# Four Silu tiles, a root and seven modulation sums moved to other places of a two-layer kernel

## The reference

```python
mod = jax.nn.silu(c) @ w_ada[l] + b_ada[l]
sh1, sc1, g1, sh2, sc2, g2 = jnp.split(mod[:, None, :], N_MOD, axis=-1)
u = rmsnorm(h, norm1_w[l]) * (1.0 + sc1) + sh1
proj = u @ w_in[l]
hq, hf, hi, hg, aq, ak, av = jnp.split(proj, offs, axis=-1)
o_hg = hgrn2(hq, hf, hi, hg, lower_bounds[l], hgrn_gnorm_w[l])   # ends: rmsnorm(o, w) * silu(hg)
o_da = diff_attention(aq, ak, av, lam, lambda_init, diff_subln_w[l])
mix = jnp.concatenate([o_hg, o_da.astype(o_hg.dtype)], axis=-1) @ w_out[l]
h = h + g1 * mix
u = rmsnorm(h, norm2_w[l]) * (1.0 + sc2) + sh2
ff = (jax.nn.silu(u @ w_ffn_gate[l]) * (u @ w_ffn_up[l])) @ w_ffn_down[l]
h = h + g2 * ff
```

## Time and profile before

| | us |
|---|---|
| median of three runs | 1548.53 |
| the profiled execution, device time | 1550.16 |
| its span | 1548.4 |
| TensorE arrays busy | 1470.0 (95%) |
| DVE busy | 984.9 (64%) |
| ACT busy | 448.9 (29%) |
| modulation sums, 80 on line 1622 (the first 16 have a line of their own) | 103.2 |

### The profile page before, as it was taken

The page is one execution under the profiler, slowest core; times in us unless marked ns, Lnnn a source line. Parts: engine busy times, 40 slices in busy tenths (PEclk is TensorE's granted clock), DMA queues, the critical chain, the costliest instruction groups (busy, mean ns, idle before and its releaser), DMA issues.

```text
span 1548.4 us, 19571 instructions
## 1 busy us (share of the span) xinstructions
PE 1470.0 (95%) x7186; PEld 1176.7 (76%) x7186; DVE 984.9 (64%) x1727; ACT 448.9 (29%) x921; POOL 95.6 (6%) x75
## 2 busy tenths in 40 slices
PE   3989999898999999998999999999998999999997
PEld 2777866576888888887876666778886888888886
DVE  8789878777676666556546666875555444444342
ACT  5333354423222221002234445531113222222011
POOL 0100000020000000221700000000030000000110
PEclk9999999998999999998999999999998999999999
DMA  9243233333655555443221111113322223233322
GB/s 368 82 155 109 68 107 111 109 110 122 203 180 201 189 192 181 143 137 122 70 82 42 42 42 42 55 49 102 109 95 68 96 94 106 84 108 88 99 88 92
DMA packets 52611, 175.80 MB, mean 114 GB/s; under 512 B 5953, under 2 KB 6337, under 8 KB 52545
## 3 DMA queue, kind: packets, MB, share of 16 engines
q1 hardware_dynamic: 52544, 174.94, 34.6%
HBM read 172.82 MB, written 2.10 MB: 113 GB/s over the span
## 4 chain that ended last, share of the span: by engine, by line
PE 51%; ACT 1%; DVE 1%; issue 0%; ACTq 0%; DVEq 0%
PE bank L623 11%; PE bank L625 11%; PE bank L624 11%; PE bank L1065 8%; PE bank L1084 2%; PE bank L1119 2%; PE bank L1096 2%; PE bank L635 1%; PE bank L636 1%; PE bank L637 1%; PE bank L996 0%; DVE wl L1602 0%; PE bank L1109 0%; PE bank L1040 0%; PE bank L732 0%
## 5 line engine op out<-in xcount | busy, mean ns | idle before, releaser
L623 PE MATMUL bank<-uh,wh 128*128 128x512 f32 x808 | 316.4, 392 | 6.0 <-DVE wl L1602 4.8
L625 PE MATMUL bank<-uh,wl 128*128 128x512 f32 x808 | 315.4, 390 | 0.0
L624 PE MATMUL bank<-ul,wh 128*128 128x512 f32 x808 | 315.3, 390 | 0.0
L1600 DVE CAST wh<-wraw 128x1024 fp32r<-128x1024 f32 (+1 forms) x235 | 156.0, 664 | 198.4 <-PE bank L625 179.7
L1602 DVE TENSOR_TENSOR wl<-wraw,wh 128x1024 fp32r<-128x1024 f32 (+1 forms) x235 | 274.0, 1166 | 8.1
L623 PEld LDWEIGHTS bank<-uh,wh 128*128 128x128 f32 x808 | 152.1, 188 | 39.0 <-issue 4.9
L624 PEld LDWEIGHTS bank<-ul,wh 128*128 128x128 f32 x808 | 152.2, 188 | 31.5
L625 PEld LDWEIGHTS bank<-uh,wl 128*128 128x128 f32 x808 | 152.1, 188 | 31.5
L623 PE MATMUL bank<-hh,wh 128*128 128x512 f32 x352 | 137.7, 391 | 0.0
L625 PE MATMUL bank<-hh,wl 128*128 128x512 f32 x352 | 137.2, 390 | 0.0
L624 PE MATMUL bank<-hl,wh 128*128 128x512 f32 x352 | 137.1, 390 | 0.0
(11 more groups left out here) (353 smaller groups left out, 2385.2 us busy)
## 6 DMA issues: line engine op xcount, KB each, us to landing
ada<-in_w_ada_dram SPq DMA_DIRECT2D x96, 512.0 KB, 4.6
wraw<-in_w_in_dram SPq DMA_DIRECT2D x61, 512.0 KB, 3.4
wraw<-in_w_ffn_gate_dram SPq DMA_DIRECT2D x44, 512.0 KB, 3.3
wraw<-in_w_ffn_up_dram SPq DMA_DIRECT2D x44, 512.0 KB, 3.3
wraw<-in_w_ffn_down_dram SPq DMA_DIRECT2D x32, 512.0 KB, 3.5
wraw<-in_w_ffn_down_dram SPq DMA_DIRECT2D x16, 384.0 KB, 3.1
wraw<-in_w_out_dram SPq DMA_DIRECT2D x16, 256.0 KB, 2.8
wraw<-in_w_out_dram SPq DMA_DIRECT2D x8, 512.0 KB, 3.3
```

The lines of the kernel that those rows point to most:

```text
L623: nc.tensor.matmul(bank[:], a, rh[:, k0 + k, :], start=(first and k == 0), stop=False)
L624: nc.tensor.matmul(bank[:], a, rl[:, k0 + k, :], start=False, stop=False)
L625: mm = nc.tensor.matmul(bank[:], b, rh[:, k0 + k, :], start=False, stop=(last and k == nk - 1))
L1600: V.tensor_copy(wh[:, slot, 0:n], wraw[:, slot, 0:n]).then_inc(w_hi, 1)
```

## The change

- The Silu of the four gate tiles, with its table load and a load of the exponential's table behind it, moves on ACT from behind the last drain of `a1` to the last head of the recurrence, ahead of exponential 7.
- The Silu of `scb[:, 1]` (the second block's `c`) moves from there to the place ahead of `ff1`.
- The square root of the head sums and its table loads move on ACT from ahead of step 0 to the end of step 1. On DVE the guard moves from step 0 to step 1, the root's reciprocal from step 1 to step 2, and the scaling of the heads from steps 2 to 5 to steps 3 to 6.
- Modulations 24 and 25 move ahead of the two last splits in the last head, 26 and 27 behind the last merge of the last head. The steps 0, 2, 4, 6 and 8 have one modulation each instead of two (28 to 32), steps 10, 12, 14 and 16 have 33 to 36 (before: two in 10, 12 and 14), and 37 to 39 go behind the splits of units 1 to 3 of `out1`. The second norm's gain moves from ahead of `out1` to its unit 5.

```diff
+        MOD_AHEAD = {PH["a1"].u0 + 13: [24], PH["da1"].u0: [25]}
+        MOD_STATES = {PH["da1"].u0 + 1: [26, 27]}
         for n_ in range(5):
-            MOD_AFTER[PH["da1"].u0 + n_ + 1] = [24 + 2 * n_, 25 + 2 * n_]
+            MOD_AFTER[PH["da1"].u0 + n_ + 1] = [28 + n_]
+        for n_ in range(4):
+            MOD_AFTER[PH["out1a"].u0 + n_] = [33 + n_]
         for n_ in range(3):
-            MOD_AFTER[PH["out1a"].u0 + n_] = [34 + 2 * n_, 35 + 2 * n_]
+            MOD_AFTER[PH["out1"].u0 + n_ + 1] = [37 + n_]
...
-                for j in MOD_AFTER.get(u - 2, ()):
+                for j in itertools.chain(MOD_AHEAD.get(u - 2, ()), MOD_STATES.get(u - 2, ()), MOD_AFTER.get(u - 2, ())):
...
                 for lv in range(1, 8):
+                    if h == HEADS1 - 1 and lv == 7:
+                        for n in range(HEADS1):
+                            A(p1[:, 12 + n, :], p1[:, 12 + n, :], ACT.Silu).then_inc(silu_ok, 1)
+                        nc.scalar.preload_act_table_set("natural_log_exp_and_others")
                     exp_level(h, lv)
...
                     a1_drain(A1_UNITS - 1)
-                    for n in range(HEADS1):
-                        A(p1[:, 12 + n, :], p1[:, 12 + n, :], ACT.Silu).then_inc(silu_ok, 1)
-                    act.wait_ge(c_land[1], 16)
-                    A(scb[:, 1, :], scb[:, 1, :], ACT.Silu).then_inc(c_silu, 1)
...
-            nc.scalar.preload_act_table(ACT.Sqrt)
-            act.wait_ge(rs_ok, 2)
-            A(rsh[:, 0:16], ssh[:, 0:16], ACT.Sqrt, bias=epst, scale=SQ_BACK / P).then_inc(rs_ok, 1)
...
                     A(p1[:, TILES["da1"][n], :], B[1][:], ACT.Copy).then_inc(drain_a, 1)
+                if m == 1:
+                    nc.scalar.preload_act_table(ACT.Sqrt)
+                    act.wait_ge(rs_ok, 2)
+                    A(rsh[:, 0:16], ssh[:, 0:16], ACT.Sqrt, bias=epst, scale=SQ_BACK / P).then_inc(rs_ok, 1)
+                    nc.scalar.preload_act_table_set("natural_log_exp_and_others")
...
             norm_u(1, mod1[:, 24:32])
+            act.wait_ge(c_land[1], 16)
+            A(scb[:, 1, :], scb[:, 1, :], ACT.Silu).then_inc(c_silu, 1)
             ffn("ff1", 0)
...
                 u = PH["a1"].u0 + n + 1
+                for j in MOD_AHEAD.get(u, ()):
+                    modulation(j)
                 split(u, u % 2)
...
                     exponents(0)
+                else:
+                    for j in (26, 27):
+                        modulation(j)
...
-                if m == 0:
+                if m == 1:
                     guard_sums(hg, 0)
...
-                if m == 1:
+                if m == 2:
                     root_sums(hg, 0)
-                if 2 <= m <= 5:
-                    head_normed(m - 2)
+                if 3 <= m <= 6:
+                    head_normed(m - 3)
...
-            v.wait_ge(mod_done, 40)
-            gains(1, mod1, vt1, NORM_B, 32)
...
                 add_out1(PH["out1"], t, OUT1_BANKS[t])
+                if t == 5:
+                    v.wait_ge(mod_done, 40)
+                    gains(1, mod1, vt1, NORM_B, 32)
```

More of the change, by code:

```diff
@@ L8 @@
+import itertools
 from contextlib import ExitStack
```

## The result

Five runs of each kernel on one chip: 1539.98 us median (1538.91 to 1542.15) after, 1548.53 (1547.54 to 1550.27) before; the ratio is 0.9946, 95% interval 0.9934 to 0.9957. Five more runs of the changed kernel gave 1540.86 and a ratio of 0.9941 (0.9927 to 0.9954). The forecast was 1538.3 in a range of 1534.5 to 1543.5, so the median came 1.7 us later than said. The profiled execution took 1538.91, with a span of 1537.2 against 1548.4.

The account below looks back on a forecast made before the run. TensorE ends the program but stalls in attention steps, on ACT at step 2 and DVE at 8, 12 and 16. Profiled 1550.16 less 10.2 gave 1540.0; on the median, 1538.3, range 1534.5 to 1543.5.

Parts of the forecast that it names:

- biased scores 7: DVE's biased scores for attention step 7, forecast to start at 245.4 instead of 251.90.
- wait at step 8: TensorE's wait ahead of step 8's output, forecast at 1.9 us instead of 2.88, with the clock falling again.
- waits at step 12: TensorE's two waits at step 12, forecast at 0.3 instead of 1.50 and 1.4 for the drain, clock staying up.
- The sum to step 16: Total gain over the attention steps up to TensorE's start at 299.37 in step 16: minus 10.2 us.
- DVE's term for step 14: Step 14's modulation is on the path; one fewer gains 1.2 us more, leaving 2.9 of wait at step 16.
- Rival 1: Only the opening is gained, fewer modulations buy nothing behind step 3: 5.9 to 6.5 us, so 1542.3; chance 0.16.
- Rival 2: The clock stays up at step 8, where half clock costs 1.8 us: gain 12.0, so 1536.5; chance 0.15.
- The terms for steps 2 and 12: Half clock expected to vanish from TensorE's stretches behind the waits of steps 2 and 12: 2.8 and 1.2 us.
- 1.2 us of cover: Idle time left on ACT behind the 4.8 us Silu block, ahead of the last head's exponential 7; block costs nothing.
- The price put on a broken cover: If ACT's idle time in the last head did not cover the Silu block, it would cost up to 4.8 us.
- Cost 0; 3.6 at most: Three modulations behind the output projection's splits fit DVE's idle time: cost 0, at most 3.6 us.
- a late unit of the output projection: Sign of being wrong: an output projection unit coming late; one late through the load queue would cost 1 to 2 us.

Follow-up runs that it names:

- collide: The kernel before with modulation 39 moved from step 14 beside GpSimd's add in the output projection, second norm's gain behind unit 5; one run, 1548.03 us.
- mods_only: The kernel before with only the modulations moved to their new places and the second norm's gain at unit 5; 1541.10 us, ratio 0.9946.
- mods_late: The changed kernel with the modulations of steps 6, 10 and 14 moved behind the splits of steps 8, 12 and 16; 1535.75 us, ratio 0.9912.
- drain_first: The changed kernel with ACT's drain of bank 1 ahead of the four squares in steps 7 and 11; 1536.13 us, ratio 0.9913.
- act_only: The changed kernel with modulations back in their old places, keeping ACT's edits, the guard's move and the norm gain at unit 5; 1546.05 us, ratio 0.9975.
- head_load: The changed kernel with two more ACT table loads behind the four Silus of the last head; 1543.89 us, ratio 0.9963; repeated, ratio 0.9964.
- out1_early: The changed kernel with two of three modulations taken out of the output projection's second half, 39 behind unit 1's split; 1538.16 us, ratio 0.9925.

## Why the forecast was right, and where it was off

In the frame of the profile before (0.72 later than the profile after):

| step | forecast | measured |
|---|---|---|
| biased scores 1 | 214.6 | 214.6 |
| drain of bank 1 starts | 217.2 | 217.3 |
| scores 3 | 221.4 | 221.5 |
| waits at steps 3 and 4 | 0.2, 0.75 | 0.20, 0.75 |
| biased scores 7 | 245.4 | 245.5 |
| wait at step 8, and from its end to the filling | 1.9, 2.1, clock falls | 1.84, 2.17, falls |
| waits at step 12 | 0.3, 1.4, clock stays | 0.29, 1.41, stays |
| wait at step 16, its end | 2.9, 289.2 | 2.88, 288.6 |

(The prediction's own terms for biased scores 7 add up to 245.5.)

**The attention steps.** Each step of the chain held, with the reasons given: who is late at which step was read from what ended the idle time, and what comes next from the rows of later steps with the same shapes. The sum to step 16 was 10.2; counted from the first scores it is 10.8, of which 0.4 is a fall of the clock at step 8 that was shorter than before's (4.70 against 5.07). DVE's term for step 14 stands alone in collide: with one modulation gone from there, the wait at step 16 is 2.87 instead of 4.07. Rival 1 is excluded by mods_only and mods_late; what it says of ACT's squares ahead of the drain holds for the second wait of steps 8 and 12 (drain_first). Rival 2 did not occur here; drain_first, mods_only and mods_late show that it was near: with waits of 1.83 alone, 1.25 and 1.02, and 0.64 and 1.02 at step 8 their clocks read 1.00 there. The terms for the clock were partly luck. Behind the four stops of before the clock reads 0.50 from 222 to 226, 256 to 260, 282 to 284 and 300 to 302. The terms for steps 2 and 12 (2.8 and 1.2 us) were read from one profile of before, whose second profile has 0.9 less at step 2; at step 12 collide has no fall (1.00 from 282 to 284) in the old order behind 1.49 and 1.41, and mods_only has one (3.26 us to the next scores instead of 1.90) behind the very waits, 0.29 and 1.41, behind which the changed kernel has none.

**The last head.** The prediction left 1.2 us of cover; it was 0.80, and the 0.4 is modulation 24: it makes the split behind it and with it the work of ACT ahead of the block 0.4 late (ACT waits 4.64 us ahead of the row at 194.31, in before 4.24 ahead of the row at 194.64), while exponential 7 comes when TensorE lets it. The prediction had that lateness, 0.5, and did not take it off the cover; act_only, without the modulation, has 1.18. Nothing was paid: TensorE's row of eight products that starts 48.9 us ahead of the first scores in before does so within 0.04 in every kernel but the two of head_load (49.3). The price put on a broken cover was one for one, with 4.8 at most; 1.8 of lateness cost 0.43 in the head and, by the timed runs, 1.7 in all. A table load took no more time than its row: in head_load the three loads of 199.34, 200.63 and 201.91 stand 1.28 to 1.29 apart, and the exponential starts 0.02 behind the last.

**The mis-sized term: the output projection.** "Cost 0; 3.6 at most" was 1.4 (from the steps' end to the norm 32.2 us instead of 30.8). I had counted DVE's three modulations at their usual 1.28 against its idle time, and not asked what runs on GpSimd in that time. The idle slot was there; the instruction in it was longer. By size it would be most of the 1.7 us by which the median missed the forecast; out1_early gives it back, and collide shows the cause. The prediction had named a late unit of the output projection as a sign of being wrong, and two came late, at 322.85 and 326.09. In the profiled pair errors of opposite sign met: the steps gave 10.7 instead of 10.2, the projection took 1.4 back, the norm gave 1.2, and 0.7 lay ahead of the steps. Its 11.2 is therefore no proof of the sum; the rows by step above are.

**The norm.** From its sum to ff1 it took 6.9 us in before's profile, 6.1 in its second, and 5.7 in both of after. The clock falls there in all of them, by the windows at about 346.6 in before (0.65 from 346 to 348) and 338.7 in after (0.68 from 338 to 340), 1.0 and 3.1 behind the norm's first row. I had no term for it. In the profiled pair it gives back 1.2 of what the projection lost (10.7 to the end of the steps, 9.2 to the norm, 10.4 to ff1). But that is no gain of the change: over the 14 profiles the stretch goes from 5.7 to 6.9 us, with 5.7 in collide, an order of before, and 6.9 in head_load_2.

What stays open: most of head_load's 3 us, whether ACT's part adds anything to the modulations in timed runs, and why the same two waits of 0.29 and 1.41 let the clock fall at step 12 of mods_only (0.50 from 274 to 276) and not in after.

## What to carry to other kernels

Idle time of an engine is a place for work only after what the other engines run in the same microseconds has been looked at: a modulation that lands beside GpSimd's add takes 2.3 us and not 1.3, and the longest duration of a group, beside its median, tells so before anything is moved. Where the profile has TensorE's clock at 0.50 behind a wait, price the wait and the half clock together: a reordering of two calls that removed 1.0 us of waiting at step 8 gave 2.7. Read that half clock from more than one profile. Free the engine that paces the next steps first: ACT's part without DVE's returned 3.5 us, DVE's without ACT's 8.5.

## What the runs showed of the hardware

A fall of TensorE's clock behind the same waits need not last the same, or come at all. In the order of before, from the filling of step 8 to scores 9, three profiles have 4.63, 5.07 and 5.96 us, and at step 12, behind 1.5 and 1.4 us of waiting, two fell (0.50 from 282 to 284 in before, 0.56 in its second profile) and one did not (1.00 in collide). Four profiles of the changed order have 4.70 to 4.86 at step 8, the two of head_load 5.70 and 6.00; with no fall (drain_first) it is 3.27. Waits of 1.83 alone (drain_first) and of 1.25 and 1.02 (mods_only) at step 8 left the clock at 1.00; behind 1.84 and 1.02 (after) it reads 0.50.

A modulation beside GpSimd's add (after, collide): 2.31 and 2.32 instead of 1.28; a cast 0.86 instead of 0.42; a subtraction 1.77 instead of 0.69, where it met the add from its start. The multiply-adds that read a PSUM bank kept their 0.75 beside the same adds (322.71 in after, beside the add from 322.47 to 323.94). A table load took 1.28 in 6 rows shown here, and where nothing else kept it waiting (behind 199.34, 200.63, 201.91 and 241.09) the instruction behind it followed within 0.02.
